# Hybrid decoder step on 8 cores: transposes of norm rows, attention outputs and k by DMA, scores of two heads in one matmul

## The reference, cut to what is computed

```python
h = _rmsnorm(x, g_mix)                                    # x: (T, 1024), T = 2048 prompt tokens + 16 meta
u, q, k, v, og, zr, ga, gb = jnp.split(h @ w_in, IN_SPLIT_IDX, axis=-1)
pool_out, new_buf = _pool_mix(u, pool_buf, ...)           # trailing windows 2, 4, 8, 16
y_a = pool_out @ w_pool_proj
o, new_S = _gla(qh, kh, vh, loga, gla_S, seg_lens)        # 4 heads, dk 64, dv 128, gated linear attention
o = o * lax.rsqrt(jnp.mean(o * o, axis=-1, keepdims=True) + EPS) * g_gla_norm
o = o * jax.nn.silu(og)
y_b = o.reshape(B, T, GLA_WIDTH) @ w_gla_proj
x = x + (jax.nn.sigmoid(ga) * y_a + jax.nn.sigmoid(gb) * y_b) @ w_out
h2 = _rmsnorm(x, g_ffn)
gate, up = jnp.split(h2 @ w_ffn_in, 2, axis=-1)           # 2816 wide each
x = x + (jax.nn.silu(gate) * up) @ w_ffn_out
y = _rmsnorm(x, g_final)
```

## Time and profile before

| | |
|---|---|
| time, median of 3 runs | 970.59 us (969.28 to 971.41) |
| the profiled execution | 971.54 us |
| its span, slowest core | 970.3 us |
| spans of the 8 cores | 960.1 to 970.3 us |
| mean granted TensorE clock | 0.990 to 0.993 |
| PE, VectorE, ScalarE, POOL busy | 908.9, 442.3, 294.4, 102.9 us |

### The profile page before, as it was taken

The page is one execution under the profiler, slowest core; times in us unless marked ns, Lnnn a source line. Parts: engine busy times, 40 slices in busy tenths (PEclk is TensorE's granted clock), DMA queues, the critical chain, the costliest instruction groups (busy, mean ns, idle before and its releaser), DMA issues.

```text
span 970.3 us, 14949 instructions; the slowest of 8 cores (960.1 to 970.3 us)
## 1 busy us (share of the span) xinstructions
PE 908.9 (94%) x5133; PEld 473.2 (49%) x5198; DVE 442.3 (46%) x724; ACT 294.4 (30%) x559; POOL 102.9 (11%) x201
## 2 busy tenths in 40 slices
PE   0999799899999899999999998999999999999996
PEld 0545466565565356545654443454444444444442
DVE  3666755555632352332235467556563242232236
ACT  2644254322542122201125531543244101101112
POOL 1400011201100021000002100111021000000001
PEclk9999999999999899999999998999999999999999
DMA  8955252434066674262534793224254451472503
GB/s 182 223 117 109 45 88 45 68 63 71 18 120 131 161 176 78 48 115 44 87 51 124 185 236 68 44 45 87 44 87 82 76 95 36 87 128 46 87 22 152
DMA packets 19097, 91.59 MB, mean 94 GB/s; under 512 B 2543, under 2 KB 3200, under 8 KB 11968
## 3 DMA queue, kind: packets, MB, share of 16 engines
q0 software_dynamic: 8784, 60.99, 37.4%
q1 hardware_dynamic: 9646, 28.98, 8.8%
q10 hardware_dynamic: 594, 0.68, 0.3%
HBM read 140.57 MB, written 11.40 MB: 157 GB/s over the span
## 4 chain that ended last, share of the span: by engine, by line
PE 82%; DMA 6%; DVE 5%; issue 3%; ACT 2%; POOL 0%; SPq 0%; DVEq 0%; ACTq 0%; POOLq 0%
PE ps L438 77%; DVE R L343 4%; DMA gss<-Sin 2%; DMA xres<-xp 2%; DMA ring<-w_a 1%; PE ps L431 1%; DMA Sin<-sgla 1%; PE ps L532 1%; PE ps L732 1%; ACT sgt L337 1%; ACT R L337 0%; PE ps L696 0%; PE ps L713 0%; PE ps L773 0%; PE ps L733 0%
## 5 line engine op out<-in xcount | busy, mean ns | idle before, releaser
L438 PE MATMUL ps<-hT,ring 128*128 128x512 bf16 (+3 forms) x2699 | 514.8, 346 | 8.7 <-ACT sgt L337 3.9
L438 PEld LDWEIGHTS ps<-hT,ring 128*128 128x128 bf16 x2728 | 262.2, 98 | 237.5 <-issue 13.2
L337 ACT ACTIVATE sgt<-ps 128x512 f32<-128x512 f32 (+3 forms) x217 | 115.0, 533 | 440.2 <-PE ps L438 369.1
L438 PE MATMUL ps<-ring,R 128*128 128x512 bf16 (+1 forms) x998 | 225.7, 382 | 7.1 <-DVE Sin L343 3.5
L343 DVE TENSOR_TENSOR R<-ps,sgt 128x384 bf16<-128x384 f32 (+2 forms) x110 | 66.3, 604 | 233.3 <-PE ps L438 220.5
L438 PEld LDWEIGHTS ps<-ring,R 128*128 128x128 bf16 (+1 forms) x1020 | 101.0, 100 | 123.5 <-issue 11.9
L343 DVE TENSOR_TENSOR xres<-xres,ps 128x512 f32<-128x512 f32 (+1 forms) x102 | 68.7, 685 | 66.6 <-PE ps L438 66.6
L438 PE MATMUL ps<-R,ring 128*128 128x384 bf16 (+2 forms) x316 | 70.9, 346 | 0.2
L339 ACT ACTIVATE R<-xres 128x1024 bf16<-128x1024 f32 (+1 forms) x43 | 45.4, 1055 | 67.4 <-DVE xres L347 40.2
L438 PE MATMUL ps<-ring,hT 128*128 128x512 bf16 (+1 forms) x271 | 64.0, 387 | 0.5
L205 POOL DMA_DIRECT2D ring<-w_f x34 | 18.5, 545 | 334.5 <-PE ps L438 333.9
(11 more groups left out here) (96 smaller groups left out, 487.2 us busy)
## 6 DMA issues: line engine op xcount, KB each, us to landing
ring<-w_f POOLq DMA_DIRECT2D x30, 1024.0 KB, 11.2
ring<-w_a POOLq DMA_DIRECT2D x24, 1024.0 KB, 11.6
xres<-xp SPq DMA_DIRECT2D x16, 512.0 KB, 22.0
y_p<-xres SPq DMA_DIRECT2D x16, 512.0 KB, 2.6
R<-xp SPq DMA_DIRECT2D x8, 512.0 KB, 6.8
ring<-w_f POOLq DMA_DIRECT2D x4, 768.0 KB, 11.7
Sin<-sgla SPq DMA_DIRECT2D x8, 256.0 KB, 6.1
gss<-Sin SPq DMA_DIRECT2D x8, 256.0 KB, 3.6
```

Of the source, the lines that this page charges most:

```text
L337: T.op('act', lambda e: e.activation(out=out, in_=in_, func=func, scale=scale, bias=bias), reads=rd, writes=wr)
L438: return [(lambda e, k=k: e.matmul(out, lhsT=lw(k), rhs=rx(k), start=(k == 0), stop=(k == K - 1))) for k in range(K)]
```

## The change

A helper `xpose` issues one transposing DMA from SP, on one of four semaphores in turn. It takes the place of PE transposes and ScalarE copies: (a) for the second norm of both passes and the rows that prepare pass 1 (`norm_t`), while the first norm of pass 0 keeps `norm_b`; (b) for `ofb` in `sD`; (c) for k, four units at once straight behind the k projection, into a larger `keTM`; unit S keeps PE. The scores of the two heads that share a key block are one matmul of 256 columns. The eight rows for pass 1 are all issued ahead of the last down projection, and `trq` holds four empty entries and then `pA`. Side steps come at every 4th tick. In pass 0 the loads of x go out from ScalarE's queue and those of the small constants from SP's.

```diff
+    keTM = bfv(R1, 12672, 8 * 256).rearrange("p (u n) -> p u n", u=8)
...
-            T.dma('sp', f'd_x{u}', [(xres[:, u, :], xp[t0:t0 + 128, :])], writes=[xres[:, u, :]])
+            T.dma('act' if p == 0 else 'sp', f'd_x{u}', [(xres[:, u, :], xp[t0:t0 + 128, :])], writes=[xres[:, u, :]])
...
+    def xpose(out, in_):
+        st['tr'] = (st['tr'] + 1) % 4
+        T.dma('sp', f"d_tr{st['tr']}", [(out, in_)], reads=[in_], writes=[out], transpose=True)
+
+    def norm_t(hb, u):
+        c0, r, us = ucol(u)
+        xpose(hT[:, :, c0:c0 + r], hb[0:r, :])
...
-    T.dma('act', 'd_id', [(cs[:, 0:128], cst[:, 0:128])], writes=[cs[:, 0:128]])
-    T.dma('act', 'd_gm', [(gmix_bc[:, :], g_mix.partition_broadcast(128))], writes=[gmix_bc[:, :]])
+    T.dma('sp', 'd_id', [(cs[:, 0:128], cst[:, 0:128])], writes=[cs[:, 0:128]])
+    T.dma('sp', 'd_gm', [(gmix_bc[:, :], g_mix.partition_broadcast(128))], writes=[gmix_bc[:, :]])
...
                     tt(keT[:, c, c0:c0 + n], ps, eiT[:, c, :], ALU.mult)
+                    if blk != 'S':
+                        u0 = c0 // 128
+                        xpose(keTM[:, u0:u0 + 4, c * 128:(c + 1) * 128], keT[:, c, c0:c0 + 512])
...
-                pe([(lambda e, h=h: e.matmul(ps[0:r, h * 128:h * 128 + r], lhsT=keT[:, h // 2, c0:c0 + r],
-                                             rhs=qeZ[:, h, c0:c0 + r], start=True, stop=True)) for h in range(4)],
+                pe([(lambda e, c=c: e.matmul(psv[:, 2 * c:2 * c + 2, 0:r], lhsT=keT[:, c, c0:c0 + r],
+                                             rhs=qeZ[:, 2 * c:2 * c + 2, c0:c0 + r], start=True, stop=True)) for c in range(2)],
...
+                if isS:
+                    bt = nbank()
+                    pt = banks_b[bt]
+                    pe([(lambda e, c=c: e.transpose(out=pt[0:r, c * 128:(c + 1) * 128], in_=keT[:, c, c0:c0 + r], identity=ident_b[:, :]))
+                        for c in range(2)], [keT[:, :, c0:c0 + r], ident_b[:, :]], [pt])
+                    act(kt[0:r, :], pt[0:r, 0:256], AF.Copy)
...
             def sD():
-                b = nbank()
-                pt = banks_b[b]
-                pe([(lambda e, h=h: e.transpose(out=pt[:, h * 128:h * 128 + r], in_=ob[0:r, h * 128:(h + 1) * 128],
-                                                identity=ident_b[0:r, 0:r])) for h in range(4)],
-                   [ob[0:r, :], ident_b[:, :]], [pt])
-                act(ofT[:, :, c0:c0 + r], pt[:, 0:512].rearrange("p (h n) -> p h n", h=4)[:, :, 0:r], AF.Copy)
+                xpose(ofT[:, :, c0:c0 + r], ob[0:r, :])
...
             if len(prev) > 1:
-                n2a(prev[-2])
-            if len(prev) > 2:
                 v = prev.pop(0)
-                norm_b(hb_of(v), v)
-        n2a(prev[-1])
+                n2a(v)
+                norm_t(hb_of(v), v)
+        n2a(prev[0])
+        norm_t(hb_of(prev[0]), prev[0])
...
-        trq = [lambda v=v: norm_b(hb_of(v), v) for v in prev]
+        trq = []
...
-        def tick(every=2):
+        def tick(every=4):
...
-                trq = [lambda v=v: norm_b(hb3[v], v) for v in range(4)]
-                for v in range(4):
-                    trq.append(lambda v=v: (norm_b(hb3[4 + v], 4 + v), pA[v]()))
+                for v in range(8):
+                    norm_t(hb3[v], v)
+                trq = [lambda: None] * 4 + pA
```

More of the change, by code:

```diff
@@ L266, in build_program @@
     attm = [sb(f"attm{i}", [128, 4, 128], BF16) for i in range(2)]
-    keTM = [sb(f"keTM{i}", [128, 256], BF16) for i in range(2)]
     keS = sb("keS", [128, 256], BF16)
@@ L316, in build_program @@
     T.split = {"qeZ", "Sf"}
-    st = {'rot': list(range(NB)), 'i': 0, 'sg': 0, 'sb': 0}
+    st = {'rot': list(range(NB)), 'i': 0, 'sg': 0, 'sb': 0, 'tr': 0}
     def nbank():
@@ L409, in load_x @@
         if u == 'S':
-            T.dma('sp', 'd_x8', [(xres[0:16, 8, :], meta[:, :]), (xres[32:96, 8, :], xs[:, :])], writes=[xres[0:96, 8, :]])
+            T.dma('act', 'd_x8', [(xres[0:16, 8, :], meta[:, :]), (xres[32:96, 8, :], xs[:, :])], writes=[xres[0:96, 8, :]])
         else:
             t0 = p * PT + u * 128
-            T.dma('sp', f'd_x{u}', [(xres[:, u, :], xp[t0:t0 + 128, :])], writes=[xres[:, u, :]])
+            T.dma('act' if p == 0 else 'sp', f'd_x{u}', [(xres[:, u, :], xp[t0:t0 + 128, :])], writes=[xres[:, u, :]])
     def nstat(xt, jk, r, us):
@@ L457, in build_program @@
     load_x(0, 'S')
-    T.dma('act', 'd_id', [(cs[:, 0:128], cst[:, 0:128])], writes=[cs[:, 0:128]])
-    T.dma('act', 'd_gm', [(gmix_bc[:, :], g_mix.partition_broadcast(128))], writes=[gmix_bc[:, :]])
+    T.dma('sp', 'd_id', [(cs[:, 0:128], cst[:, 0:128])], writes=[cs[:, 0:128]])
+    T.dma('sp', 'd_gm', [(gmix_bc[:, :], g_mix.partition_broadcast(128))], writes=[gmix_bc[:, :]])
     for u in range(8):
         load_x(0, u)
-    T.dma('act', 'd_wgk', [(wgk_s[:, :], w_gk[:, :])], writes=[wgk_s[:, :]])
-    T.dma('act', 'd_ps', [(pscale_c[:, :], pscale[:, :])], writes=[pscale_c[:, :]])
-    T.dma('act', 'd_gn', [(gn_bc[:, :], g_gn.partition_broadcast(128))], writes=[gn_bc[:, :]])
+    T.dma('sp', 'd_wgk', [(wgk_s[:, :], w_gk[:, :])], writes=[wgk_s[:, :]])
+    T.dma('sp', 'd_ps', [(pscale_c[:, :], pscale[:, :])], writes=[pscale_c[:, :]])
+    T.dma('sp', 'd_gn', [(gn_bc[:, :], g_gn.partition_broadcast(128))], writes=[gn_bc[:, :]])
     T.dma('sp', 'd_cs', [(cs[:, 128:NCS], cst[:, 128:NCS])], writes=[cs[:, 128:NCS]])
@@ L686, in gla @@
             am = attm[bi]
-            kt = keS if isS else keTM[bi]
+            kt = keS if isS else keTM[:, u, :]
             ob = ofb[bi]
@@ L695, in sA1 @@
                 ps = banks[b]
-                pe([(lambda e, h=h: e.matmul(ps[0:r, h * 128:h * 128 + r], lhsT=keT[:, h // 2, c0:c0 + r],
-                                             rhs=qeZ[:, h, c0:c0 + r], start=True, stop=True)) for h in range(4)],
+                psv = ps[0:r, :].rearrange("p (h n) -> p h n", h=4)
+                pe([(lambda e, c=c: e.matmul(psv[:, 2 * c:2 * c + 2, 0:r], lhsT=keT[:, c, c0:c0 + r],
+                                             rhs=qeZ[:, 2 * c:2 * c + 2, c0:c0 + r], start=True, stop=True)) for c in range(2)],
                    [keT[:, :, c0:c0 + r], qeZ[:, :, c0:c0 + r]], [ps[:, :]])
[L699 to L702, removed]
                 mk = cs[0:r, C_MAS:C_MAS + SR] if isS else cs[0:r, C_MA:C_MA + 128]
-                tt(am[0:r, :, 0:r], ps[0:r, :].rearrange("p (h n) -> p h n", h=4)[:, :, 0:r],
-                   mk.unsqueeze(1).to_broadcast([r, 4, r]), ALU.mult)
-                act(kt[0:r, :], pt[0:r, 0:256], AF.Copy)
+                tt(am[0:r, :, 0:r], psv[:, :, 0:r], mk.unsqueeze(1).to_broadcast([r, 4, r]), ALU.mult)
+                if isS:
[4 more added lines that the diff above has]
+                    act(kt[0:r, :], pt[0:r, 0:256], AF.Copy)
             def sB1():
```

## The result

The changed kernel takes 976.44 us (median of 5) against 970.59 us: 0.63% slower, ratio 1.0063, 95% interval [1.0033, 1.0093]. The forecast was 953. One execution of each fell far above the rest and is left out of the comparison.

The account below looks back on a forecast made before the run. PE's instruction stream, busy 94% of the span, was taken as the bound. Slots -16.5, last attention output -3.9, sample states -4, added wait +1.5, start +5 sum to -17.9: 970.59 to 953 us, range 946 to 991.

Parts of the forecast that it names:

- Slots removed: PE's transposes of norm rows (11.0 us), attention outputs (3.7) and k (1.8) leave its stream: -16.5 us.
- pairing: Scores as two matmuls of 256 columns instead of four of 128: slot stays 0.22 us, taken as 0.
- The start: Large constants run beside x in pass 0, taking bandwidth ahead of x1: +5 us, between 0 and +8.
- about 5 us later: Sign to check: landing of x1 and issue of slab 1, against 22.4 and 24.70 us before.
- Price of a transpose: L, DMA time per norm row one after another: 3.6 us, 2.7 for half a row; none late at 3.6.
- every bound I set: Upper bound on L for a norm row, if written in pieces of 32 bytes: 8.4 us.
- 8L - 32.4: Lateness at pass 1's second norm: eight rows at L each, against FFN block B's start; not late at L = 3.6.
- Last attention output: PE's wait for `ofb` and its low clock vanish in pass 0 (-3.9 us); pass 1 waits longer for ofT (+1.5).
- unit 7 was asked for only 8 us later: Pass 0: PE goes on to block Y's gate first, needing unit 7 some 8 us later, so no wait.
- Sample states: Side steps at every 4th tick cover the store and load that PE waited on: -4 us, between 0 and -5.
- The rivals: Slow transposes past break-even (0.28; 991 at L = 6), start for nothing (948, 0.13), start 8 with sample-state stall (960).
- break-even: In the slow-transposes rival, the L from which late rows decide the result: 5.2 us.

Follow-up runs that it names:

- e2: Kernel before with only the queues of the first loads changed (x of pass 0 on ScalarE's, constants on SP's): 984.97 us, ratio 1.0146.
- e1: Changed kernel with the first loads back on their old queues, all DMA transposes kept: 960.47 us, ratio 0.9902 to the kernel before.
- e7: Changed kernel with its own start queues, but SP's large constants wait for the last row of x: 961.71 us, ratio 0.9921 to the kernel before.
- e5: e1 with the two slab loads released at the output projection's end held until the last transpose into hT lands: 952.37 us, ratio 0.9826 to the kernel before.
- e8: Kernel before with side steps at every 4th tick and nothing else: 967.06 us, ratio 0.9968.
- e10: e9 with side steps at every 2nd tick: 962.76 us, ratio 0.993 to the kernel before.
- e9: e5 with the first two loads of sample states issued ahead of the output projection: 953.76 us, ratio 0.9833 to the kernel before.
- e4: e1 with side steps at every 2nd tick again: 970.06 us, ratio 0.9994 to the kernel before.
- e6: e5 with the attention output of each pass's last unit transposed by PE again: 951.93 us, ratio 0.9826 to the kernel before.
- e12: e6 with the first two loads of sample states issued ahead of the output projection: 950.89 us, ratio 0.9804 to the kernel before.

## Why the prediction was wrong

- *Slots removed, -16.5*: right. No gap is left where the transposes stood, the estimate by busy time and clock gives 17.0, and pairing is worth 0 in the slot.
- *The start, +5, range 0 to +8*: the step that failed first. It cost 14.1 us (e2) and gave back 16.0 when undone (e1). That the large constants take their share beside x was right, and e7 shows it. The path was wrong. I divided the bytes of the constants by the rate of all engines and let the lag act on x1 and slab 1, "about 5 us later". Slab 1 went out 0.7 us later on the core shown (24.0 to 27.6 us on the eight cores, 22.8 to 24.7 before). What held PE were the rows behind: from slab 1 on, the slabs, released by statistics and not by need, compete for x5 to x7, which land at about 40, 48 and 55 us. The last row came 44.47 us after its issue; in e7 it had landed at 31.18, so the lag of x reached 24 us.
- *Price of a transpose, L = 3.6 us*: 3.1 us alone, 2.3 to 2.4 for half a row, and for rows transposed alone no lateness is seen. Wrong was to use one L for all. The last row of the second norm goes out beside slab loads in both passes, since the slabs are released exactly there, and lands after 11.6 to 14.0 us on the cores of the changed kernel, past every bound I set (8.4). The formula 8L - 32.4 was wrong too: it runs all eight rows from the first one's time, while the last row has only its own slack, 9.0 us in pass 1. With the two slab loads held back (e5) the wait is gone and the kernel 7 to 8 us faster, of which 5 to 6 can be placed there.
- *Last attention output, -3.9 in pass 0 and +1.5 in pass 1*: the saving did not come. In pass 0 two slab loads went out at 193.02 us. The transposes of the last two units, issued at 194.50 and 201.21, took 17.0 and 10.8 us and landed together, near 212 (14.1 and 8.1 us on core 3, say). I had said that unit 7 was asked for only 8 us later; PE asked for it at 207.78, 6.6 us after its issue, and waited 4.63. Over both passes PE waits 3.4 to 8.9 us for `ofT` on the eight cores, where it waited 4.3 for `ofb` on each core of the kernel before.

```profile
R<-ofb SPq DMA_TRANSPOSE x1, 17.0
```
```profile
201.21 10.80 DMA R<-ofb
...
212.41 1.33 PE L446 MATMUL ps<-R,ring 128*128 128x352 bf16 x4 [4.63 <-DMA R<-ofb]
```

- *Sample states, -4*: right in direction, -2.7 in the kernel before (e8), 9.0 and 9.6 with the transposes (e10 against e9, e4 against e1). In e4 the wait is that of the first state load, late behind the transposes and beside slabs, with some 2.6 us lost to the lower clock. With that load early (e10) the cost stays, at a later load beside slabs. Why it stays at 9 us there, with waits for Sin of 2.0 to 5.2, is open.
- *The rivals*: that slow transposes lose the gain was told with its break-even, at L = 5.2 for all of them. It came in another form, a price three to seven times as high for the one or two rows beside slab loads, and by itself it did not lose it: without the start the change gains 10 us (e1). No rival had a start that costs more than 8. The sum as it stood: -17.9 forecast; the start was short by 9 to 11, the rest by 12.5 (-10.4 measured in e1 against -22.9), of it 7 to 8 with the slabs held behind the last row (e5 against e1). For the 5 us left, the waits for `ofT` are the largest new ones that the traces show, but doing the last row by PE left most of the waiting in place (e6) and gained about 3 us with early state loads (e12 against e9), so this part is argued and not shown.

## What to carry to other kernels

What is needed first must stand first in one queue, or the other transfers must wait for it: two queues that ran side by side here kept no order between them (e2, e7). A small transfer put beside a large one can be paid at the price of the large one, so look for what else is released at the same point of the program, and hold that back if it has slack; one dependency was worth 7 to 8 us here. In this kernel, bound by PE, a transpose by DMA paid where its row had more slack than a slab load takes. Give each row its own deadline, above all the last one before a consumer. Holding the slab back was the cure that worked here; PE for the last row alone gained nothing (e6).

## What the runs showed of the hardware

- A transpose by DMA, SBUF to SBUF, of 128 x 1024 bf16 took 3.1 us from issue to landing, 0.39 us for each 128 x 128 block. It held SP's queue for 1.23 us in e5, and for 2.87 in the changed kernel beside slab loads. The Trainium skill (VectorE: DVE Perf Modes, "The three transpose paths") gives 1309 ns per block; by these runs a row of eight takes far less than eight times that; a single block was not run. Advanced Engine Details and Errata, "X-Bar Transpose (TRN2)", says that such transfers are as fast as regular ones; the 3.6 us of a regular transfer of the same 256 KB agree with that.
- The same transfer beside two slab loads of 1 MB and 0.75 MB took 13.1 us on the core shown, and 11.6 to 14.0 us over the eight cores and both passes. Half a row (an attention output) took 2.3 us alone and 13.0 to 17.0 us when issued just after two slab loads of 1 MB in pass 0.
- PE transposes of 128 x 128 cost 55 ns each in a stream, at full clock.
- Behind PE's waits of 4.34 us (changed kernel, 748.80) and 6.82 us (e4, 282.86) the granted clock was 0.50 (1.2 GHz) for the next 4.0 and 5.2 us. By half of these stretches such a wait costs an estimated 2.0 and 2.6 us more.
